# Three groups instead of two by seven products in each half of the down projections

## What is computed

```
def swiglu(x, w_gate, w_up, w_down):
    return (jax.nn.silu(x @ w_gate) * (x @ w_up)) @ w_down

h = swiglu(rms_norm(x, ffn1_pre_g[l]), ffn1_w_gate[l], ffn1_w_up[l], ffn1_w_down[l])
x = x + 0.5 * rms_norm(h, ffn1_post_g[l])
```

## Time and profile before

| | |
|---|---|
| median of three runs | 1765.66 us (1764.64 to 1766.03) |
| profiled execution | 1764.84 us, its span 1763.2 us |
| granted TensorE clock | 0.998 of full speed |
| TensorE matmul busy | 1738.4 us, 99% |
| VectorE busy | 1411.3 us, 80% |
| ScalarE busy | 1000.9 us, 57% |
| GpSimd busy | 64.3 us, 4% |
| DMA | 389.75 MB, mean 221 GB/s |

### The profile page before, as it was taken

How to read it: one execution, slowest core, us unless ns; L and a number is a source line. 1 busy time by engine, 2 the same in 40 slices (tenths; PEclk the granted TensorE clock), 3 DMA queues, 4 the chain that set the end, 5 groups by cost and what they waited for, 6 DMA issues and landing times. The chain is left out here.

```text
span 1763.2 us, 21394 instructions
## 1 busy us (share of the span) xinstructions
PE 1738.4 (99%) x7968; PEld 1442.9 (82%) x7968; DVE 1411.3 (80%) x1284; ACT 1000.9 (57%) x979; POOL 64.3 (4%) x99
## 2 busy tenths in 40 slices
PE   9999999999999999999999999999999999999998
PEld 8788888888888888888888877788888888888886
DVE  6888888888888888665578558888888888888887
ACT  6656665555655654543347446555566666555563
POOL 0000000000000000010000000000000000000000
PEclk9999999999999999999999999999999999999999
DMA  9677787777765554355441446777777787666453
GB/s 387 224 264 250 253 261 244 238 238 241 243 236 220 188 214 176 137 225 189 175 162 52 188 174 255 262 239 238 245 251 241 251 251 244 233 235 239 170 195 112
DMA packets 58978, 389.75 MB, mean 221 GB/s; under 512 B 6432, under 2 KB 6688, under 8 KB 16160
## 3 DMA queue, kind: packets, MB, share of 16 engines
q1 hardware_dynamic: 52720, 344.77, 50.9%
q0 software_dynamic: 6048, 44.04, 13.0%
q10 hardware_dynamic: 144, 0.04, 0.0%
HBM read 384.63 MB, written 4.19 MB: 221 GB/s over the span
## 5 line engine op out<-in xcount | busy, mean ns | idle before, releaser
L2084 PE MATMUL banks<-w_hi,act_hi 128*128 128x512 f32 (+1 forms) x1088 | 425.2, 391 | 1.6 <-DVE w_lo L1343 1.2
L2086 PE MATMUL banks<-w_hi,act_lo 128*128 128x512 f32 (+1 forms) x1088 | 421.5, 387 | 0.0
L2085 PE MATMUL banks<-w_lo,act_hi 128*128 128x512 f32 (+1 forms) x1088 | 421.2, 387 | 0.0
L1384 DVE TENSOR_TENSOR op_lo<-quads,op_hi 128x2048 fp32r<-128x2048 f32 x140 | 318.7, 2289 | 43.1 <-ACT op_hi L918 42.2
L918 ACT ACTIVATE op_hi<-quads 128x2048 fp32r<-128x2048 f32 x140 | 266.6, 1918 | 53.8 <-PE banks L2086 33.7
L2278 PE MATMUL banks<-w_hi,hid_split 128*128 128x512 f32 x992 | 275.1, 389 | 0.5 <-DVE hid_split L1607 0.5
L1373 DVE TENSOR_TENSOR w_lo<-raw,w_hi 128x2048 fp32r<-128x2048 f32 x80 | 181.4, 2288 | 80.9 <-ACT w_hi L892 80.7
L1343 DVE TENSOR_TENSOR w_lo<-raw,w_hi 128x2048 fp32r<-128x2048 f32 (+3 forms) x67 | 143.9, 2147 | 124.7 <-ACT w_hi L843 124.7
L2084 PEld LDWEIGHTS banks<-w_hi,act_hi 128*128 128x128 f32 x1088 | 204.6, 188 | 43.4 <-DVE w_lo L1343 2.2
L2086 PEld LDWEIGHTS banks<-w_hi,act_lo 128*128 128x128 f32 x1088 | 204.3, 188 | 41.8
L2085 PEld LDWEIGHTS banks<-w_lo,act_hi 128*128 128x128 f32 x1088 | 204.7, 188 | 40.0
(11 more groups left out here) (209 smaller groups left out, 2331.3 us busy)
## 6 DMA issues: line engine op xcount, KB each, us to landing
raw<-in_weights SPq DMA_DIRECT2D x203, 1024.0 KB, 4.9
quads<-in_paired SPq DMA_DIRECT2D x80, 1024.0 KB, 7.8
quads<-in_paired POOLq DMA_DIRECT2D x40, 1024.0 KB, 8.4
raw<-in_paired SPq DMA_DIRECT2D x32, 768.0 KB, 6.0
rows<-in_x SPq DMA_DIRECT2D x4, 1024.0 KB, 11.7
raw<-in_weights SPq DMA_DIRECT2D x6, 512.0 KB, 3.6
gain_row<-in_post_gains SPq DMA_DIRECT2D x3, 1024.0 KB, 6.5
raw<-in_weights SPq DMA_DIRECT2D x4, 768.0 KB, 4.1
```

Source lines behind the costliest of these rows:

```text
L1384: nc.vector.tensor_tensor(op_lo[:, slot, :], op_raw(op), op_hi[slot][:, :], ALU.subtract)\
L2084: nc.tensor.matmul(out_ap, hi, rhs_hi, start=start, stop=False, skip_group_check=chain)
L2085: nc.tensor.matmul(out_ap, hi, rhs_lo, start=False, stop=False, skip_group_check=chain)
L2086: return nc.tensor.matmul(out_ap, lo, rhs_hi, start=False, stop=stop, skip_group_check=chain)
```

## The change

Each half has 13 pieces and three groups: `DP` is 26, `D_GROUPS` 6, `D_STEPS` 42. With 21 products for 13 pieces, a table says how many products stand behind each piece, by down projection and half. There are two operand buffers; they lie over `rows`, whose reload moves behind their last use. Two of the four weight sums of a group are made by transfers that GpSimd issues: R12 + R11 with its source in DRAM, and R11 + R22 from SBUF to SBUF. The signs of sums are turned so that a transfer, which can only add, will do; `sum_sides` gets a fifth instruction for this, and two of the end's additions become subtractions. Where SyncE waited for a VectorE sum ahead of R22's load it now waits for the second transfer.

```diff
-DP = 32
+DP = 26
-D_GROUPS = 4
+D_GROUPS = 6
+GAPS = {(0, 0): (1,) + (2,) * 9 + (1, 1, 0), (0, 1): (2,) * 9 + (1, 1, 1, 0),
+        (1, 0): (1,) + (2,) * 9 + (1, 1, 0), (1, 1): (2,) * 10 + (1, 0, 0)}
+def products_behind(down, half, p):
+    first = D_HALF * half + sum(GAPS[down, half][:p])
+    return range(first, first + GAPS[down, half][p])
+def product_slot(down, n):
+    half, k = n // D_HALF, n % D_HALF
+    return 0 if half and not down and k == D_HALF - 2 else k % 2
...
-        op_split = sb("op_split", [P, 2, D_OPERAND], F32R)
+            op_split = sb("op_split", [P, 2, 2, D_OPERAND], F32R, s)
+        sb("op_split_at", [P, 2, D_OPERAND])
```

SyncE, in each half (the load of a piece stays behind the same wait):

```diff
+                        for n in products_behind(down(stage), half, p):
+                            load_behind(stage, n)
+                        if half and p == HALF - 3:
+                            sp.wait_ge(down_used, down_step(stage, last_in_slot1(down(stage))))
+                            for t in range(TILES):
+                                load_rows_again(stage, t)
...
+                if op == O_P7:
+                    sp.wait_ge(down_lo_ready, down_step(stage, n))
+                    sp.wait_ge(down_sum2_landed, down_step_sum(stage, group))
+                    load_down_quad(stage, group + 1, R22)
```

GpSimd, once per half and stage:

```diff
+            def add_down_quads(stage, half):
+                for group in range(D_GROUPS // 2 * half, D_GROUPS // 2 * (half + 1)):
+                    row = 8 * (UNITS - 1) + 4 * (D_GROUPS * down(stage) + group) + R11
+                    pool.wait_ge(down_sum_ready, down_sum(stage, group, 1))
+                    nc.gpsimd.dma_start(down_quad(R12), paired[row, :, 0:D_OPERAND]
+                                        .rearrange("p (a n) -> p a n", a=D_PAIRS), accum_op=ALU.add)\
+                      .then_inc(down_sum1_landed, 16)
+                    nc.gpsimd.dma_start(down_quad(R11), down_quad(R22), accum_op=ALU.add).then_inc(down_sum2_landed, 16)
```

ScalarE, for the operand of a product:

```diff
-                    act.wait_ge(down_used, down_step(stage, n - 1))
+                if slot_used_by(down(stage), n) is not None:
+                    act.wait_ge(down_used, down_step(stage, slot_used_by(down(stage), n)))
...
+                        act.wait_ge(down_sum1_landed if op == O_P5 else down_sum2_landed, down_step_sum(stage, group))
```

VectorE:

```diff
-            def down_sum1():
...
-            def down_sum2(stage, group):
...
             def down_sum4(stage, group):
-                dve.wait_ge(down_sum_ready, down_sum(stage, group, 3))
+                dve.wait_ge(down_sum2_landed, down_step_sum(stage, group))
...
+                for half in range(2):
+                    for p in range(HALF):
+                        ahead = HALF * half + p + 1
...
+                        if plain:
+                            take_low_down(pc)
+                        for i, n in enumerate(products_behind(down(stage), half, p)):
+                            if n % D_HALF:
+                                down_operand_low(stage, n)
+                            if n % D_HALF == D_HALF - 1:
+                                end_second(stage, half)
+                            if plain and i == 0:
+                                hid_low_down(stage, pc, ahead)
+                            if n % D_HALF == D_HALF - 1:
+                                if final:
+                                    take_low_last(down_piece_of(DOWN2, DP - 1))
+                                end_third(stage, half)
+                            behind_operand(stage, n)
...
+                    if half == 0:
+                        side_low(stage, D_GROUPS // 2, SIDE_A11)
+                        down_operand_low(stage, D_HALF)
+                        take_both_down(stage, HALF)
...
+                        for t in range(TILES):
+                            scale_down(0, sums_before, t)
+                        take_both_down(stage, HALF + 1)
```

TensorE:

```diff
+                    for p in range(HALF):
+                        if not (stage == DOWN2 and half and p >= HALF - 2):
+                            down_piece(stage, HALF * half + p, mixed if not half and not p else None)
+                        if half == 0 and p == 1:
+                            turn_hidden(gu_stage, N_FB - 1)
+                        for n in products_behind(down(stage), half, p):
+                            down_product(gu_stage, stage, n)
```

More of the change, by code:

```diff
@@ L494, in down_sum, with down_step_sum @@
         def down_sum(stage, group, k):
-            return 4 * (D_GROUPS * down(stage) + group) + k
+            return 2 * (D_GROUPS * down(stage) + group) + k
+        def down_step_sum(stage, group):
+            return 16 * (D_GROUPS * down(stage) + group + 1)
         def side(stage, group, k):
@@ L686, in load_down_stage, with load_behind @@
                             load_down(stage, HALF + k + 2)
[L687 to L704, removed]
+            def load_behind(stage, n):
+                group, op = down_group(n), D_ORDER[n % len(D_ORDER)]
+                if group == D_GROUPS - 1:
+                    return
+                if op == O_P7:
+                    sp.wait_ge(down_lo_ready, down_step(stage, n))
+                    sp.wait_ge(down_sum2_landed, down_step_sum(stage, group))
+                    load_down_quad(stage, group + 1, R22)
+                elif op == O_P5:
+                    sp.wait_ge(down_lo_ready, down_step(stage, n))
+                    load_down_quad(stage, group + 1, R12)
+                elif op == O_P6:
+                    sp.wait_ge(down_sum_ready, down_sum(stage, group, 2))
+                    sp.wait_ge(down_lo_ready, down_step(stage, n))
+                    load_down_quad(stage, group + 1, R11)
+                elif op == O_P4:
+                    sp.wait_ge(down_lo_ready, down_step(stage, n))
+                    load_down_quad(stage, group + 1, R21)
             def load_mix_first():
@@ L778, in step, with inverse_rms @@
                 pool.wait_ge(var_ready, steps[0])
[L780 removed]
+            def inverse_rms(job, parts, width, factor, col=0, run=None):
                 c = factor ** -2
[L784 removed]
+                for n in range(parts) if run is None else run:
                     for t in range(TILES):
@@ L817, in _ @@
             add_all_quads(GU1)
-            inverse_rms(R_POST1, 2, D, 0.5)
+            for half in range(2):
+                add_down_quads(DOWN1, half)
+                inverse_rms(R_POST1, 2, D, 0.5, run=(half,))
             inverse_rms(R_PRE_MIX, 1, D, 1.0)
@@ L1122, in down_proj @@
                 gate_mixed(gu_stage, N_FB - 1, part0, per_unit(gu_stage, UNITS - 1, 4, 3))
[L1123 to L1145, removed]
@@ new lines, in down_proj @@
+                for half in range(2):
+                    for p in range(HALF):
+                        ahead = HALF * half + p + 1
+                        plain = 1 <= p < HALF - 1 and not (stage == DOWN2 and ahead == DP - 1)
+                        if plain:
+                            take_high_down(down_piece_of(stage, ahead))
+                        for i, n in enumerate(products_behind(down(stage), half, p)):
+                            if n % D_HALF:
+                                down_operand_high(gu_stage, stage, n)
+                            if plain and i == 0:
+                                hid_high_down(down_piece_of(stage, ahead), ahead)
+                            if n == 2:
+                                keep_hidden(gu_stage, N_FB - 2, N_FB - 1)
+                            behind_operand(stage, n)
+                        if plain and not products_behind(down(stage), half, p):
+                            hid_high_down(down_piece_of(stage, ahead), ahead)
+                    if half == 0:
+                        down_operand_high(gu_stage, stage, D_HALF)
@@ L2286, in down_product @@
                 group, op, half = down_group(n), D_ORDER[n % len(D_ORDER)], n // D_HALF
+                slot = product_slot(down(stage), n)
                 pe.wait_ge(down_lo_ready, down_step(stage, n))
```

195 lines of the change are left out of this document (97 added, 98 removed).

## The result

The kernel after took 1809.04 us (median of 4 runs, 1807.46 to 1811.31), the kernel before 1765.22 beside it (4 runs): ratio 1.0245, interval 1.023 to 1.0261. It is slower by some 44 us where I had said 4 to 5 and a range up to 1776. The direction was right, and it would have been without the transfers (experiment 1), but the size was wrong by a factor of nine to ten.

A forecast was written before the change was run, and what follows sets the result against it. TensorE, busy 99% of the span, was taken to bound the down projections. The terms -8.2 + 4.9 + 3.9 + 1.2 + 2.7 + 0.6 = +5.1 us, on 1764.84, gave 1770 us, range 1762 to 1776.

The forecast's parts named there:

- The 36 matmuls: Four halves of the down projections have 501 matmuls each instead of 510: 8.2 us less on TensorE's path.
- A: Start of each down projection: a fifth sides' sum instruction and a late operand for the third product; 4.9 us.
- D: Tail of the last half: VectorE waits at the end's first addition, so the last operand is late; 2.7 us.
- The walk: Block-by-block reckoning of VectorE's queue against TensorE: ordinary blocks hold, five kinds of places don't.
- E: GpSimd's two adding transfers: first lands at 6.8 us, pair at 11.3; 0.6 us, bounds 0 and 13.
- B: Between a down projection's halves: first piece 1.4 us late, 1.0 more than before, second product 0.95; 3.9 us in all.
- C: From first down projection to the mixer: first input pieces load behind the last operand; 1.2 us, bounds 0 and 2.4.
- Rival 1: Down projections: only the sums of work count, VectorE's reserve covers crowded places, nothing is lost; 1756.6 us, chance 0.14.
- Rival 3: Tail and transition to the mixer are hidden and cost nothing; 1766 us, no change, chance 0.18.
- Rival 2: Adding transfers: the pair lands at 13 us or later and costs 7.4 us or more; 1777 us, chance 0.13.

The follow-up runs named there:

- experiment 1: Changed kernel without both adding transfers (two operands per group not right), waiters released by VectorE's sum of R22: 1769.67 us against 1766.31 for the kernel before.
- experiment 2: Changed kernel with 1920 instead of 1024 bytes per partition for descriptors of GpSimd's transfers: 1798.23 us against 1766.31 for the kernel before.
- Experiments 7 and 8: Both experiment 2 with one change: 7 moves SyncE's R22 load behind R11's, 1791.82 us; 8 cuts R11's load to 32 of 1536 columns, 1792.4 us.
- experiment 3: Changed kernel with R11 + R22 made by VectorE and one adding transfer per group left: 1771.58 us against 1766.31 for the kernel before.

## Why the prediction was wrong, step by step

**The 36 matmuls and A to D: right.** The walk without E summed to +4.5 us, and experiment 1 has +3.4. A put 2.0 us ahead of the third product: 493.51 + 0.23 to 495.44 is 1.70. B put 1.4 and 0.95 at the second half: 593.72 + 2 x 0.2267 to 595.55 is 1.38, and the next bracket has 0.61, with the 0.2 of modelled ends 0.8. D had VectorE idle for some 6 us ahead of the end's first addition and then 2.1 us of TensorE: 6.48 and 2.00. Its further 0.6 and part of C did not show: the transition to the mixer has 2.21 + 1.32 = 3.5 us of idle TensorE against 0.97 + 1.72 = 2.7 before, 0.8 where I took 1.2. What the earlier trace rows gave as pitches of an in-order queue was good to a few tenths of a microsecond at each place.

**E: the step that failed.** "I estimate the first by size at 6.8 and the pair at 11.3: the second has to follow behind in the same queue", at 0.6 us. It cost 39. The rule that the step used, that a landing is free up to 11.0, 12.8 and 11.5 us in groups 0, 2 and 4 and costs TensorE what is beyond, came out about right in its sums. The landing put into it was wrong, and other waiters were left out. In the order of their size:

First, the landing of the pair, 11.3. With 15.4, the median measured in the kernel after, the same rule gives 2 x (4.4 + 2.6 + 3.9) = 22 us. TensorE's stalls ahead of the sixth and seventh products of these groups are 20.6 us in 10 places, 22.6 with 0.2 more at each. Two that have not been shown yet, sixth products of groups 0 and 2 in the kernel after:

```profile
513.85 0.50 PE L2159 MATMUL banks<-op_split,sums_hi 128*128 128x512 f32 x1 [1.74 <-DVE op_split L1692]
...
588.49 0.50 PE L2159 MATMUL banks<-op_split,sums_hi 128*128 128x512 f32 x1 [1.94 <-DVE op_split L1692]
```

With the 13.6 of experiment 2 the rule gives 2 x (2.6 + 0.8 + 2.1) = 11, and there it is the four seventh products, 11 us. Two things made the landing late. One is the issue. I had GpSimd issue both at once, and it waits 6.0 to 8.4 us for descriptor room in between. Experiment 2 prices this at 11 us. In the trace of before GpSimd's two adding transfers of a block pair are issued 9 us apart (230.03 and 239.09), the second behind a wait for VectorE, so that no row showed it.

The other is the second's own time: 6.8 + 6.2 (experiment 2) and not 6.8 + 4.5. Two transfers one behind the other in one queue should have been taken at twice the one, 13.6. A fit in the Trainium skill ("DMA: Bandwidth & Descriptors", the SWDGE anatomy) gives 768 KB 3.8 us. The runs have 6.8 for an adding transfer alone, and the measurement decides: the trace of before, with 7.9 for 1 MB, was the better guide, as the prediction held.

Second, only one waiter had a price, VectorE's last sum. The text also named ScalarE's split for the fifth product (for the first transfer) and SyncE's loads, and gave them nothing. It did not name a fourth: ScalarE's split for the sixth product waits for the second transfer, 42.6 us in 11 places. TensorE's other stalls that the transfers brought are some 8 us in 10 places, 10 with the 0.2 at each. Experiments 7 and 8 put 6 us of such stalls on SyncE's wait and the bunch of loads behind it; the rest is open.

Third, the clock, 6 to 7 us. Behind the stalls at 518.71 (2.50 us), 588.49 (1.94) and 1581.77 and 1586.63 (2.44 and 1.89) TensorE ran for some microseconds at the lower level; the prediction had no term for this.

**The rivals.** Rival 1 (only the sums count, 1757) is refuted by experiment 1: the 2.0 us at the third product are there without any transfer. Rival 3 (C and D hidden) is refuted by the same stalls. Rival 2 had the mechanism and its sign ("a group 0 whose last sum comes 13 us behind the sum of R22": it came after 16.0), but its 1777 took the landing at 13 and left out the same waiters as E.

**What stays open.** Of the 28.5 us that the pair costs with room for both, 11 are the four seventh products, 6 SyncE's wait with its bunch of loads and 3 to 4 the granted clock (0.994 against 0.996 in the spans of experiments 2 and 1). Of the clock only some 1.7 us stand behind a stall of the pair, the one at 1734.50. Two stretches with as much lie outside the down projections, where the pair doesn't run (the third value from the end is the granted clock):

```profile
1064.00:1070.00 6.00, 5.99 (x25) 4.61 (x26) 5.70 (x9) 3.14 (x8) 0.00 (x0) 0.72 0.06 26
1149.00:1155.00 6.00, 6.00 (x20) 4.78 (x21) 6.00 (x6) 2.88 (x4) 0.00 (x0) 0.72 0.91 307
1734.00:1740.00 6.00, 5.50 (x18) 4.48 (x19) 4.64 (x4) 3.04 (x3) 0.00 (x0) 0.72 0.89 300
```

The rest, 7 to 8 us, are, as far as the trace shows them, stalls of 0.2 to 1.2 us ahead of other products. Whether ScalarE's wait for the second transfer (25.5 us in 9 places in experiment 2) or VectorE's causes them, no run separates, as one semaphore releases both. SyncE's loads of quarters also land later beside the pair (median 6.4 us in experiment 2, 5.5 in experiment 1), and no run prices that apart. Nor was the pair tried with the second transfer issued later and its consumer moved back by a block.

## What to carry to other kernels

A wait that is new on several in-order queues has to be priced on each of them, down to the loads that it releases late and in a bunch for the next round; comparing the landing with the reserve of one consumer is not enough. Of two adding transfers issued together, count the second as landing after the sum of both times, and look whether the descriptor area holds both. Where one engine still has room in its sum, as VectorE had 33 us of work per 38 of TensorE, one more instruction of 1.67 us there can be cheaper than a transfer that takes it away: here 1771.6 against 1809.0, and with a table that spaces the products, 1760.0 against 1765.5 of the kernel before.

## What the runs showed of the hardware

- GpSimd stands still at the issue of a 768 KB adding transfer while the one ahead of it is under way, with 1024 bytes per partition for descriptors (6.0 to 8.4 us); with 1920 bytes it issues it 0.5 to 0.8 us behind the first. The profile calls that wait "issue" and shows no releaser.
- Two adding transfers of 768 KB in flight show no overlap: the first lands 6.8 us after its issue, as fast as alone (6.9, experiment 3), the second 13.0 from SBUF and 13.5 from DRAM (one run).
- A load of 768 KB issued 2.6 us behind a bunch of three others took 7.8 us to land; with two of them out over 6 us ahead and the third behind it, 4.4 (experiments 2 and 7, one place). A load of 16 KB behind the three took 5.5 us there (experiment 8).
- Stalls of TensorE of 1.9 to 2.5 us are followed in some places, not in all, by matmuls at 1.2 GHz (the granted clock is 0.72 in 516 to 522, with 2.50 us, and in 588 to 594, with 1.94; it is 1.00 in 1747 to 1752, with 2.50 us as well).
